# Keys of the differential attention computed transposed, the reduction of the sine's arguments moved, and eleven turn slots merged

## The reference, cut to what matters

```
# differential attention, 8 heads, two maps m of 64 columns each
q, k, v = split(rmsnorm(h, attn_norm) @ w_in, 3)
logits = einsum('bqhmd,bkhmd->bmhqk', q, k) * scale + bias      # causal
p = softmax(logits); attn = p[:, 0] - lam * p[:, 1]
o = rmsnorm(attn @ v, subln_w) @ w_out

# mLSTM: Sc = (q k^T) * exp(D - m_j), then Sc @ v
# retention: rq, rk = rope(...), scores = (q k^T) * decay, o = scores @ v
# latent attention: q and k split in a part "nope" of 128 and a part "rope" of 64 for 8 heads,
#   rope(x, pos) = x * cos(pos*inv), x * sin(pos*inv), paired
# hybrid: mixed = sigmoid(gr) * (ro * silu(rg)) @ w_br + sigmoid(gm) * (mo @ w_bm)
```

## Time and profile before

| | us |
|---|---|
| median of 3 runs | 1143.27 |
| lowest, highest | 1143.17, 1143.4 |
| the profiled execution | 1142.95 |
| its span | 1141.1 |
| PE busy in it | 1135.7 |
| DVE busy | 758.5 |
| ACT busy | 628.2 |

### The profile page before, as it was taken

The page is one execution under the profiler, slowest core; times in us unless marked ns, Lnnn a source line. Parts: engine busy times, 40 slices in busy tenths (PEclk is TensorE's granted clock), DMA queues, the critical chain, the costliest instruction groups (busy, mean ns, idle before and its releaser), DMA issues.

```text
span 1141.1 us, 15933 instructions
## 1 busy us (share of the span) xinstructions
PE 1135.7 (100%) x5732; PEld 957.3 (84%) x5732; DVE 758.5 (66%) x1034; ACT 628.2 (55%) x965; POOL 65.6 (6%) x81
## 2 busy tenths in 40 slices
PE   9999999999999999999999999999999999999998
PEld 6878888888888888888898887888888888888887
DVE  6987666556684766656679879665755667566565
ACT  7696554445568555435456465666644455354344
POOL 3001100000000100000030042000000000000000
PEclk9999999999999999999999999999999999999999
DMA  9644566665555566656567555444656556666542
GB/s 316 185 147 130 175 194 187 193 191 186 171 162 161 158 196 193 196 184 193 177 184 227 175 170 166 133 126 126 179 187 202 180 171 188 196 188 195 190 155 104
DMA packets 99557, 203.49 MB, mean 178 GB/s; under 512 B 7917, under 2 KB 19845, under 8 KB 99504
## 3 DMA queue, kind: packets, MB, share of 16 engines
q1 hardware_dynamic: 98160, 199.68, 56.2%
q0 software_dynamic: 1184, 3.04, 0.9%
q10 hardware_dynamic: 160, 0.07, 0.0%
HBM read 201.70 MB, written 1.06 MB: 178 GB/s over the span
## 4 chain that ended last, share of the span: by engine, by line
PE 97%; ACT 1%; DVE 1%; issue 0%
PE pair L775 17%; PE pair L777 16%; PE pair L776 16%; PE pair L907 8%; PE turn_ps L907 8%; PE score L776 4%; PE score L777 4%; PE score L775 4%; PE pair L905 3%; PE turn_ps L905 3%; PE turn_ps L808 3%; PE pair L1231 3%; PE pair L1229 1%; ACT da_e L1553 1%; PE turn_ps L910 0%; PE pair L910 0%
## 5 line engine op out<-in xcount | busy, mean ns | idle before, releaser
L1910 DVE TENSOR_TENSOR w_lo<-raw,w_hi 128x1024 fp32r<-128x1024 f32 (+3 forms) x379 | 454.7, 1225 | 167.3 <-ACT w_hi L1428 166.2
L1428 ACT ACTIVATE w_hi<-raw 128x1024 fp32r<-128x1024 f32 (+3 forms) x379 | 389.3, 1051 | 211.6 <-DMA raw<-in_mlp_w 69.6
L775 PE MATMUL pair<-w_hi,a_both 128*128 128x512 f32 (+3 forms) x464 | 184.4, 397 | 0.0
L777 PE MATMUL pair<-w_hi,a_both 128*128 128x512 f32 (+3 forms) x464 | 178.4, 384 | 0.0
L776 PE MATMUL pair<-w_lo,a_both 128*128 128x512 f32 (+3 forms) x464 | 177.9, 383 | 0.0
L907 PE MATMUL pair<-a_both,w_hi 128*128 128x512 f32 x384 | 141.9, 394 | 0.0
L907 PE MATMUL turn_ps<-a_both,w_hi 128*128 128x512 f32 x384 | 141.9, 394 | 0.0
L777 PEld LDWEIGHTS pair<-w_hi,a_both 128*128 128x128 f32 x464 | 87.1, 188 | 17.4
L775 PEld LDWEIGHTS pair<-w_hi,a_both 128*128 128x128 f32 x464 | 87.3, 188 | 15.9 <-ACT work L1473 0.3
L776 PEld LDWEIGHTS pair<-w_lo,a_both 128*128 128x128 f32 x464 | 87.4, 188 | 15.3 <-issue 0.2
L905 PE MATMUL pair<-a_both,w_lo 128*128 128x256 f32 x336 | 93.8, 279 | 0.0
(11 more groups left out here) (443 smaller groups left out, 1841.2 us busy)
## 6 DMA issues: line engine op xcount, KB each, us to landing
raw<-in_mlp_w SPq DMA_DIRECT2D x128, 512.0 KB, 3.6
raw<-in_w_in SPq DMA_DIRECT2D x64, 512.0 KB, 3.7
raw<-in_w_up SPq DMA_DIRECT2D x32, 512.0 KB, 3.7
raw<-in_w_down SPq DMA_DIRECT2D x32, 512.0 KB, 3.3
raw<-in_mlstm_w_in SPq DMA_DIRECT2D x24, 512.0 KB, 4.1
raw<-in_attn_w_in SPq DMA_DIRECT2D x23, 512.0 KB, 5.8
raw<-in_w_br SPq DMA_DIRECT2D x16, 512.0 KB, 4.2
raw<-in_attn_w_out SPq DMA_DIRECT2D x8, 512.0 KB, 3.3
```

What stands on the lines that cost most here:

```text
L775: pe.matmul(o, hi, whi, start=start, stop=False)
L777: return pe.matmul(o, lo, whi, start=False, stop=stop)
L1428: act.activation(w_hi[:, k % RING, 0:n], raw[:, k % RING, 0:n], ACT.Copy).then_inc(hi_ready, 1)
L1910: dve.tensor_tensor(w_lo[:, k % RING, 0:n], raw[:, k % RING, 0:n], w_hi[:, k % RING, 0:n], ALU.subtract).then_inc(lo_ready, 1)
```

## The change

**Keys.** The 1024 key columns of the differential attention are four groups of 256 columns, k0 to k3, with two units each, computed by `turned_dense` (formerly `ret_dense`) and so transposed as they come. The order of groups is q0, k0, k1, q1, k2, k3, v0, v1; the unit numbers of q1, v0 and v1 stay. A unit of a key group is read from memory as 128x4x256 numbers in place of 128x2x512. Gone are the 16 transposes of keys, ACT's four emptying copies and its four copies to `da_k`. New are: four ACT copies `k_low` (128x512), four DVE additions `sum_key` (128x512), four DVE multiplications `scale_key` (128x512) by the rows' factor, which now has to lie along the free axis and so is spread by POOL (`row_cols`, 128x256), turned by PE ("rowT", two transposes) and copied by ACT. `setup_slot` still stands after unit 6 on PE, now with the rowT turn in it.

**Sine.** `angles` moves on DVE from after unit 10 to after unit 12, `reduced_angles` from after unit 11 to after unit 22. ACT's `angle_slot` moves one unit later, and the copy of the last keys comes ahead of it. The scores, exponents, `da_pair` and `da_end` keep their place among the units.

**Slots.** Work of two neighbouring slots is put in one, at the same number of instructions: the transposes of `roT` in gm0 and gm1 (8 slots to 4), those of the latent queries (4 to 3) and keys (4 to 2, and 2 to 1), the retention's scores (4 to 2) and the mLSTM's scores and values (4 to 3). PE has 11 slots fewer there. ACT's and DVE's part follows.

```diff
-    for name, col in (("q0", 0), ("k0", D), ("q1", HALF), ("k1", D + HALF), ("v0", 2 * D), ("v1", 2 * D + HALF)):
-        group(name, qkv, col, HALF, "x0", DC, 2, 0)
+    for name, col in (("q0", 0), ("k0", D), ("k1", D + S), ("q1", HALF), ("k2", D + 2 * S), ("k3", D + 3 * S),
+                      ("v0", 2 * D), ("v1", 2 * D + HALF)):
+        if name[0] == "k":
+            group(name, qkv, col, S, "x0", DC, 1, 1, per=4)
+        else:
+            group(name, qkv, col, HALF, "x0", DC, 2, 0)
...
 # PE
-            dense("k0", {2: setup_slot})
-            qk_turns("q0", 0)
-            dense("q1", {1: lambda: qk_turns("k0", 1), 2: lambda: (da_score(0), da_score(1))})
-            dense("k1", {1: lambda: (da_score(2), da_score(3)), 3: lambda: qk_turns("q1", 0)})
-            dense("v0", {1: lambda: qk_turns("k1", 1), 2: lambda: (da_score(4), da_score(5)),
-                         3: lambda: (da_probs(0), da_probs(1))})
...
-            dense("mo0", {0: lambda: ml_score(0), 1: lambda: ml_score(1), 2: lambda: (ml_score(2), ml_value(0)),
-                          3: lambda: (ml_score(3), ml_value(1))})
+            dense("mo0", {1: lambda: (ml_score(0), ml_score(1)), 2: lambda: (ml_value(0), ml_score(2)),
+                          3: lambda: (ml_value(1), ml_score(3))})
...
-            dense("gm0", {n: (lambda n=n: ro_turn(2 * n)) for n in range(4)})
-            dense("gm1", {n: (lambda n=n: ro_turn(8 + 2 * n)) for n in range(4)})
+            dense("gm0", {1: lambda: ro_two(0), 3: lambda: ro_two(4)})
+            dense("gm1", {1: lambda: ro_two(8), 3: lambda: ro_two(12)})
...
 # ACT
+            def copy_key(n):
+
+                wait_group(act, f"k{n}")
+                act.wait_ge(group_dve, groups[f"k{n}"]["dve_end"] - 1)
+                act.activation(k_low[:, :, :], group_ps(f"k{n}")[:, :, S:], ACT.Copy).then_inc(group_act, 1)
...
-            dense("v0", {0: angle_slot, 1: lambda: copy_heads("k1", da_k, 4),
-                         3: lambda: (da_exp(4), da_probs(0), da_probs(1))})
+            copy_key(3)
+            dense("v0", {1: angle_slot, 3: lambda: (da_exp(4), da_probs(0), da_probs(1))})
...
 # DVE
-            dense("k0", {0: angles, 1: reduced_angles, 2: setup_slot})
+            def sum_key(n):
+
+                dve.wait_ge(group_act, groups[f"k{n}"]["act_end"])
+                if n:
+                    dve.wait_ge(da_keyed, n)
+                dve.tensor_tensor(k_sum[:, :, :], group_ps(f"k{n}")[:, :, 0:S], k_low[:, :, :], ALU.add)\
+                    .then_inc(group_dve, 1)
+
+            def scale_key(n):
+
+                dve.wait_ge(turn_act, turn["rowT"]["act_end"])
+                dve.wait_ge(group_dve, groups[f"k{n}"]["dve_end"])
+                dve.tensor_tensor(da_k[:, 2 * n:2 * n + 2, :], k_sum[:, :, :], spread_to(row_t[:, :], 1, [2, S]),
+                                  ALU.mult).then_inc(da_keyed, 1)
+
+            dense("k0")
+            sum_key(0)
+            dense("k1", {0: lambda: (angles(), setup_slot(), scale_key(0))})
+            sum_key(1)
+            scale_key(1)
...
             dense("q1", {2: lambda: da_pair(0), 3: lambda: da_end(0)})
-            dense("k1", {0: lambda: da_end(1), 1: lambda: da_pair(2), 2: lambda: da_end(2), 3: lambda: da_end(3)})
-            dense("v0", {2: lambda: da_pair(4), 3: lambda: da_end(4)})
+            dense("k2", {0: lambda: da_end(1), 1: lambda: da_pair(2)})
+            sum_key(2)
+            dense("k3", {0: lambda: (da_end(2), scale_key(2)), 1: lambda: da_end(3)})
+            sum_key(3)
+            scale_key(3)
+            dense("v0", {0: reduced_angles, 2: lambda: da_pair(4), 3: lambda: da_end(4)})
...
 # POOL
+            pool.wait_ge(rstd_ready, 1)
+            pool.tensor_copy(row_cols[:, :, :], rstd[:, 0, :].unsqueeze(2).to_broadcast([P, TT, P])).then_inc(row_spread, 1)
```

More of the change, by code:

```diff
@@ L249, in turns @@
             order.append((f"{name}n{b}", 1, 0))
-            if name == "mq" and b >= 2:
-                order.append((f"mqr{b - 2}", 0, 1))
-        if name == "mk":
-            order.extend([(f"mkr{b}", 0, 1) for b in range(2)])
+        order.extend([(f"{name}r{b}", 0, 1) for b in range(2)])
     for h in range(MLA_H + 1):
@@ L1021, in setup_slot @@
                 transposed("gains", [gain_rows[:, :]])
+                pe.wait_ge(row_spread, 1)
+                transposed("rowT", [row_cols[:, tt, :] for tt in range(TT)])
                 pe.wait_ge(lam_sum, 1)
@@ L1029, in _, with turned_dense, unit, qk_turns @@
             warm(2)
-            def qk_turns(name, n):
-                if n == 0:
-                    pe.wait_ge(flip_loaded, 16)
+            def turned_dense(name, slots=None):
+                ps = open_pair(name)
+                def unit(u):
+                    k, c0, n = u
+                    pe.wait_ge(lo_ready, k + 1)
+                    for j in range(n):
+                        c = c0 + j
+                        for b in range(2):
+                            cols = slice((2 * j + b) * P, (2 * j + b + 1) * P)
+                            if c:
+                                pe.matmul(ps[:, b, S:], w_lo[:, k % RING, cols], a_hi[:, c, :],
+                                          start=False, stop=False)
+                            last = pe.matmul(ps[:, b, :], w_hi[:, k % RING, cols], a_both[:, c, :, :],
+                                             start=c == 0, stop=c == DC - 1)
+                            if c == 0:
+                                last = pe.matmul(ps[:, b, S:], w_lo[:, k % RING, cols], a_hi[:, c, :],
+                                                 start=False, stop=False)
+                    last.then_inc(unit_used, 1)
+                run_group(name, unit, slots)
+            def qk_turns(name):
+                pe.wait_ge(flip_loaded, 16)
                 pe.wait_ge(group_act, groups[name]["act_end"])
                 for half in range(2):
-                    cols = [qk_sb[:, n, tt, (2 * half + j) * P:(2 * half + j + 1) * P]
+                    cols = [qk_sb[:, tt, (2 * half + j) * P:(2 * half + j + 1) * P]
                             for j in range(2) for tt in range(TT)]
-                    transposed(f"{name}{'ab'[half]}", cols, ident if n else flip)
+                    transposed(f"{name}{'ab'[half]}", cols, flip)
             def da_score(h):
@@ L1822, in _, with copy_two @@
             ret_squares(0)
-            dense("rv2", {n: (lambda n=n: mla_copy("mq", n)) for n in range(4)})
+            def copy_two(which, b):
+                mla_copy(which, b)
+                mla_copy(which, b + 1)
+            dense("rv2", {1: lambda: copy_two("mq", 0), 2: lambda: copy_two("mq", 2)})
             empty_value(2)
@@ L1827, in _ @@
             scores_hi(2)
[L1828 removed]
+            dense("rv3", {1: lambda: copy_two("mk", 0), 3: lambda: copy_two("mk", 2)})
             empty_value(3)
```

123 lines of the change are left out of this document (67 added, 56 removed).

## The result

| | before | changed |
|---|---|---|
| median of 7 runs, us | 1143.4 | 1147.34 |
| lowest, highest | 1143.12, 1144.19 | 1146.59, 1149.9 |
| ratio to before, 95% interval | | 1.0036 (1.0026 to 1.0045) |
| span of the profiled execution | 1141.1 | 1145.5 |

The changed kernel is slower by 3.9 us. The forecast was 1145.0 with a range up to 1147.0, so the time lies outside it, and clearly on the slower side where "within 0.2%" had most of the chance.

What follows compares the result with a forecast made beforehand. PE's row of matmuls was taken to bound the kernel, busy 1135.7 of 1141.1 us. Profiled 1142.95 +2.23 (keys and sine) -0.5 (slots) is +1.7; with the median 0.3 above the profiled one, 1145.0, range 1142.2 to 1147.0.

Steps and rivals of the forecast that it cites:

- within 0.2%: Whole kernel: the case that the measurement can't be told from no change, 1141.0 to 1145.6 us; chance 0.57.
- The chain of DVE and ACT: First logits to exponents of head 4: DVE's queue, then the sine and exponents on ACT, set PE's time; 2.23 us later.
- PE's wait at the turn: At the turn of the first probabilities, PE waits from 71.85 for DVE to read the logits of heads 4 and 5: 3.3 us.
- PE's wait at the scores of head 4: Before heads 4 and 5, PE's 0.56 us wait for ACT's copy of the turned keys goes away.
- At no cost: POOL's 128x256 copy, ACT's changed copies and key units in smaller pieces were counted as nothing.
- the clock: After PE's wait at 71.85, the granted clock drops from the 2.4 to the 1.2 GHz level: 2.0 us; chance 0.08.
- merged slots, -0.5: Eleven fewer PE slots at 0.04 us each, gaining 0.5 us, from 0 to 1.1.
- I count no new wait: At the merged slots, ACT's and DVE's lead of six units was taken to cover later copies, so no wait was added.
- 2.23: Keys and sine together: exponents of head 4 start at 76.12 instead of 73.89, and all of the 2.23 us reaches PE.
- Rival 2: The clock falls in PE's 3.3 us wait at 71.85, costing 2.0 us: 1147.0 us; chance 0.08.
- Rival 3: Longer chain: four key sums and scales take 0.96 us, not 0.61, +1.4, or slower transfers up to 1 us: 1146.3; chance 0.12.

Runs made afterwards that it cites:

- the kernel with 14 dummies: The changed kernel with 14 dummy matmuls of 512 columns on PE ahead of its turn of the first probabilities: 1146.31 us.
- the gap: The changed kernel with `reduced_angles` behind head 0's softmax end on DVE and the sine ahead of the exponents of heads 2 and 3: 1143.09 us.
- in front: The changed kernel with `reduced_angles` put back ahead of the first logits on DVE, behind the angles: 1145.64 us.
- on a neighbour engine: The changed kernel with `reduced_angles` on POOL instead of DVE, the sine ahead of the exponents of heads 2 and 3: 1145.63 us.
- a sister kernel: The changed kernel with the reduction on POOL, retention's scores merged: 1145.63 us; the profile compared with it has those scores single again, 1145.58 us.

## Why the prediction was wrong

**The chain of DVE and ACT was right, link by link.**

| | forecast | measured |
|---|---|---|
| first scores | 40.8 | 41.08 |
| first logits | 41.8 | 42.16 |
| logits of head 2 | 54.20 | 54.55 |
| reduction done | 70.34 | 70.66 |
| logits of head 4 | 73.35 | 73.64 |
| PE's wait at the turn | 3.3 | 3.21 |
| exponents of head 4 | 76.12 | 76.41 |

The times all lie 0.3 us late, and 0.24 of it was there at 16 us, where the profiles of all these kernels differ by 0.7 (16.23 to 16.97). The durations taken from the rotation held: 0.61 for the sum, 0.79 where the scale waits for it. PE's wait at the scores of head 4 went away. "At no cost" held for POOL's copy and the key units' transfers as far as the first logits tell.

**Step that failed: the clock.** I priced the fall at 2.0 us and gave it 0.08, since no row of before showed a wait of PE over 0.56 us. A trace that has no long wait says nothing about what happens after one, and the forecast itself made one of 3.3 us. The nine slow matmuls at the start of the program were the only row on PE after more than 0.56 us of idleness, and they were slow, though the granted clock reads 1.00 there. That was evidence for the rival, and its chance should have been much larger. The runs showed a granted clock of 0.50 behind the wait and 1.6 us more on PE, where I had 2.0. Of the 1.6 about 1.0 was not hidden by ACT's chain.

**Step that failed: merged slots, -0.5.** It came out as nothing (1.0001); by places the sum is within 0.1 of nothing with the slots alone and +0.2 in the changed kernel. The price of a slot was right for the transposes. "I count no new wait" was wrong. I looked for who waits for the moved copies, and not for what PE's moved work had been covering: a score between two groups is time for ACT to empty a bank.

**Not in the sum:** the late unit at 602 us, 0.8 us in the profiled run, whose cause is open, and the 0.24 us of the start.

For the profiled execution the forecast's sum is 1142.95 + 2.23 - 0.5 = 1144.7. With +0.24 for the start, +1.0 for the clock, +0.7 for the slots and +0.8 for the late unit it is 1147.4; measured 1147.34. The 1.0 is what the kernel with 14 dummies gave back, the others are read from the places above.

The range was too narrow for another reason: it took the rivals one at a time. Rival 2 is no alternative to the forecast's wait but follows from it, so a time near 1146, and not 1145.0, should have been the middle, and 1147.0 not the end. (Rival 3's own sum, 1145.0 + 1.4, is 1146.4 and not 1146.3.)

The Trainium skill ("TensorE: Matmul & The Clock Gate", Part 1) says that the throttled state is the default and activity releases it. These traces agree: 0.50 granted behind 3.21 us of idleness, back at 1.00 from 79 us. Of its other statement, N / 2.4 GHz plus 2.5 ns between matmuls, the traces show 0.23 us at 512 columns here too, not 0.216.

## What to carry to other kernels

When a forecast contains a wait of the matmul engine that is longer than any in the trace, its price is the wait and perhaps a low clock behind it. Behind 3.2 us it was low in both profiles, behind 2.2 us in the only one. Behind 1.3 us it stayed up in three profiles and fell in one, after two more waits in the 10 us ahead. Dummy matmuls bought the low clock's 1.0 us back. Before work is moved on the critical engine, list what it covers: the moved score was time in which ACT emptied a bank. And a step in a full queue is best put into a gap that the trace shows. Against the gap, it cost 2.5 us more in front, 2.5 on a neighbour engine and 4.2 behind.

## What the runs showed of the hardware

- The clock need not fall at once: after 2.22 us of idleness six transposes and two matmuls ran at full speed, and behind a third that was in between seven started 0.42 to 0.43 us apart, with PE busy all along.
- The clock can fall after a wait of 1.33 us: in one profile nothing but waits of 0.71, 0.86 and 1.33 us stood within 10 us, and the granted clock was 0.50 behind the last; with 0.56, 0.86 and 1.33 us in a sister kernel it stayed at 1.00.
- Elementwise work of POOL on 128x640 float32 stretched DVE's instructions beside it: three low parts took 5.37 us for 3.50, one scale 1.53 for 0.69, the same in both profiles. A sum that reads one operand from PSUM kept its 0.68.
